# Compressor products with 128 moving columns, and the first block's projections from rows not yet normalised

## The reference, cut to what matters

```python
def first_block(x, norm1_g, w_in, ...):
    for i in range(DEPTH):                       # DEPTH = 2
        h = rmsnorm(x, norm1_g[i])
        mix = hybrid_mixer(h, w_in[i], cmp_pos[i], cmp_w1[i], cmp_w2[i], ...)
        x = x + mix @ w_out[i]
        h = rmsnorm(x, norm2_g[i])
        x = x + conv_glu_ffn(h, w_up[i], ...)
    return rmsnorm(x, final_g)
```

## Time and profile before

| | |
|---|---|
| median of 3 runs (lowest, highest) | 1905.39 us (1905.17 to 1916.05) |
| profiled execution, span from first to last instruction | 1924.8 us |
| time around that span | not shown; the profile has the span alone |
| mean granted PE clock in it | 0.986 |
| PE, PEld, DVE, ACT busy | 98%, 90%, 70%, 50% |
| records of all engines | 31636 |

### The profile page before, as it was taken

The page is one execution under the profiler, slowest core; times in us unless marked ns, Lnnn a source line. Parts: engine busy times, 40 slices in busy tenths (PEclk is TensorE's granted clock), DMA queues, the critical chain, the costliest instruction groups (busy, mean ns, idle before and its releaser), DMA issues.

```text
span 1924.8 us, 31636 instructions
## 1 busy us (share of the span) xinstructions
PE 1879.2 (98%) x12720; PEld 1726.5 (90%) x12720; DVE 1354.0 (70%) x2154; ACT 958.4 (50%) x1429; POOL 110.6 (6%) x112
## 2 busy tenths in 40 slices
PE   8999999999999999999999999999999999999998
PEld 6888999888899999999888989998999898989997
DVE  5566878745777787677877877777776777875445
ACT  5556444645654445434754454345343565454433
POOL 0000000000000000000001401100110001400100
PEclk9989999997999999999999999999999999999999
DMA  7215777541367777776431157875786442035552
GB/s 286 70 63 197 262 270 292 183 155 66 110 244 284 280 262 278 281 267 221 158 127 67 62 212 279 307 276 213 278 302 226 150 138 103 1 132 198 196 202 82
DMA packets 54510, 374.45 MB, mean 195 GB/s; under 512 B 6016, under 2 KB 6656, under 8 KB 12800
## 3 DMA queue, kind: packets, MB, share of 16 engines
q1 hardware_dynamic: 51808, 362.34, 51.3%
q0 software_dynamic: 2304, 9.93, 1.5%
q10 hardware_dynamic: 288, 0.65, 0.1%
HBM read 371.84 MB, written 1.05 MB: 194 GB/s over the span
## 4 chain that ended last, share of the span: by engine, by line
PE 87%; DVE 7%; ACT 4%; issue 1%; DMA 0%; SPq 0%; DVEq 0%; ACTq 0%
PE bank L707 14%; PE bank L709 14%; PE bank L708 14%; PE bank L870 6%; PE bank L871 6%; PE bank L872 6%; PE bank L783 3%; PE bank L784 3%; PE bank L785 3%; PE bank L1348 2%; DVE w_lo L1988 2%; PE bank L1358 1%; PE bank L1056 1%; PE bank L833 1%; PE bank L1025 1%
## 5 line engine op out<-in xcount | busy, mean ns | idle before, releaser
L1988 DVE TENSOR_TENSOR w_lo<-raw,w_hi 128x2048 fp32r<-128x2048 f32 (+4 forms) x279 | 607.8, 2182 | 76.4 <-ACT w_hi L1446 76.0
L707 PE MATMUL bank<-hT_hi,w_hi 128*128 128x256 f32 x2304 | 654.1, 284 | 2.0 <-DVE scratch L2747 2.0
L708 PE MATMUL bank<-hT_lo,w_hi 128*128 128x256 f32 x2304 | 651.8, 283 | 0.0
L709 PE MATMUL bank<-hT_hi,w_lo 128*128 128x256 f32 x2304 | 651.8, 283 | 0.0
L1446 ACT ACTIVATE w_hi<-raw 128x2048 fp32r<-128x2048 f32 (+4 forms) x268 | 502.1, 1875 | 147.5 <-PE bank L872 116.2
L707 PEld LDWEIGHTS bank<-hT_hi,w_hi 128*128 128x128 f32 x2304 | 440.1, 191 | 8.9 <-issue 6.5
L708 PEld LDWEIGHTS bank<-hT_lo,w_hi 128*128 128x128 f32 x2304 | 440.2, 191 | 2.8 <-issue 0.5
L709 PEld LDWEIGHTS bank<-hT_hi,w_lo 128*128 128x128 f32 x2304 | 440.2, 191 | 0.2
L870 PE MATMUL bank<-w_hi,hid_hi 128*128 128x512 f32 x528 | 206.7, 392 | 1.1 <-DVE hid_lo L2064 0.8
L871 PE MATMUL bank<-w_lo,hid_hi 128*128 128x512 f32 x528 | 206.2, 391 | 0.0
L872 PE MATMUL bank<-w_hi,hid_lo 128*128 128x512 f32 x528 | 205.4, 389 | 0.0
(11 more groups left out here) (410 smaller groups left out, 2451.2 us busy)
## 6 DMA issues: line engine op xcount, KB each, us to landing
raw<-in_wb SPq DMA_DIRECT2D x158, 1024.0 KB, 4.9
raw<-in_wa SPq DMA_DIRECT2D x94, 1024.0 KB, 4.9
scratch<-in_wm SPq DMA_DIRECT2D x72, 1024.0 KB, 7.0
raw<-in_wb SPq DMA_DIRECT2D x8, 940.0 KB, 4.7
raw<-in_wb SPq DMA_DIRECT2D x4, 936.0 KB, 4.7
lnw<-in_ln_g POOLq DMA_DIRECT2D x6, 512.0 KB, 5.0
lnw<-in_ln_b POOLq DMA_DIRECT2D x6, 512.0 KB, 6.1
scratch<-in_c SPq DMA_DIRECT2D x5, 512.0 KB, 3.7
```

The lines of the kernel that those rows point to most:

```text
L707: nc.tensor.matmul(out, ah, bh, start=(i == 0), stop=False)
L708: nc.tensor.matmul(out, ah, bl, start=False, stop=False)
L709: last = nc.tensor.matmul(out, al, bh, start=False, stop=(i == n - 1))
L1988: return nc.vector.tensor_tensor(w_lo[:, slot, cols], raw[:, raw_slot, cols], w_hi[:, slot, cols].bitcast(F32), ALU.subtract)
```

## The change

1. The compressor's first products take 128 moving columns in place of 30. The operand is a window of 128 columns of `rw`, which holds 32 x 30 columns side by side; the 30 that are wanted come first in it (for the last few products the window is clamped and the output shifted). The output window lies so that the wanted sums gather at columns 68 to 97 of the bank.
2. In the first block's input projection PE turns x and not `xn`; ACT's copies out of the banks multiply by the row factor. `rms_tile` of both row tiles moves on ACT from ahead of the first turned tiles to behind the splitting of both tiles for chunks 0 and 1, and so ahead of hi(2). DVE no longer writes `xn` there.
3. At the start of the program x is loaded by row tile, chunk 0 in two halves, and ACT and DVE split chunk 0 in four quarters; 18 idle transposes are dropped, 10 stay. The table of small parameters is loaded in three parts.
4. Between the layers, PE turns the first row tile two tiles of the sweep earlier, and the 8 idle transposes are dropped. The table load for the root at the end of layer 0 is dropped too.
5. The last chunk's copy out is two instructions of 256 columns and no longer one of 512. Some semaphores are merged.

```diff
@@ sync (SP): start of the program
-            sp.dma_start(x[:, :, :], t["x"].rearrange("o (t p) d -> p (o t) d", p=P)).then_inc(x_in, 16)
             sp.dma_start(cst[:, 0:P], t["const"][:, 0:P]).then_inc(x_in, 16)
+            sp.dma_start(x[:, 0, :], rows_of_x[:, 0, :]).then_inc(x_in, 16)
+            sp.dma_start(spa[:, 0:KT], t["sa"][0, :, 0:KT]).then_inc(small_in, 16)
+            sp.dma_start(raw[:, 0, 0:2 * HW], t["wa"][0, 0, :, 0:2 * HW]).then_inc(open_in, 16)
...
+                    if (l, n) == (0, 0):
+                        sp.dma_start(raw[:, 0, 2 * HW:CW], t["wa"][0, 0, :, 2 * HW:CW]).then_inc(raw_in[0], 16)
+                        sp.dma_start(x[:, 1, :], rows_of_x[:, 1, :]).then_inc(row_in, 16)
+                        continue
@@ tensor (PE): sweep, start of a layer, compressor
-                            if (i, half, f) == (1, 1, FT - 1) and turn_first is not None:
+                            if (i, half, f) == (1, 1, FT - 3) and turn_first is not None:
...
                 if l == 0:
-                    idle_turns(0, 18)
-                    pe.wait_ge(A["xn"], due(A, "xn", 1))
-                    turn_tile(A, xn, 0, 1)
+                    turn_tile(A, x, 0, 1)
+                    idle_turns(0, 10)
 
                 def turn_next():
-                    pe.wait_ge(A["xn"], due(A, "xn", 2 * TT + 2))
-                    turn_tile(A, xn, 0, 1)
+                    pe.wait_ge(A["x"], summed(l, 0, 1))
+                    turn_tile(A, x, 0, 1)
 
                 def turn_second():
-                    pe.wait_ge(A["xn"], due(A, "xn", TT))
-                    turn_tile(A, xn, 1, 1)
-
-                if l == 0:
-                    idle_turns(0, 10)
-                else:
-                    idle_turns(0, 8)
+                    if l == 0:
+                        pe.wait_ge(row_in, 16)
+                    else:
+                        pe.wait_ge(A["x"], summed(l - 1, 1, 1))
+                    turn_tile(A, x, 1, 1)
...
+                        elif l:
+                            pe.wait_ge(A["x"], summed(l - 1, 1, i))
...
-                        last = nc.tensor.matmul(G[0][:, 0:2 * NCMP], raw[:, n % RING, (first + jj) * P:(first + jj + 1) * P],
-                                                rw[:, j, :], start=(j == 0), stop=(j == CBLK - 1))
+                        at = min(j * 2 * NCMP, CBLK * 2 * NCMP - P)
+                        to = HID_AT - (j * 2 * NCMP - at)
+                        last = nc.tensor.matmul(G[0][:, to:to + P], raw[:, n % RING, (first + jj) * P:(first + jj + 1) * P],
+                                                lent[0][:, at:at + P], start=(j == 0), stop=(j == CBLK - 1), skip_group_check=True)
@@ scalar (ACT): start of a layer, copies out
                 if l == 0:
-                    hi_a(0)
-                    rms_tile(NEXT, 1, 3, lambda i, half: None)
                     act.wait_ge(small_in, 16)
-                    hi_tile(A, 0, 0, "g1", range(KH))
-                    hi_a(1)
-                    hi_tile(A, 0, 1, "g1", range(KH))
-                else:
-                    act.wait_ge(A["x"], summed(l - 1, 1, 0))
-                    square(NEXT, 1, 0)
-                    half_mean(NEXT, 1, 6 * l + 4)
-                    hi_tile(A, 0, 0, "g1", range(0, 2))
-                    act.wait_ge(A["x"], summed(l - 1, 1, 1))
-                    square(NEXT, 1, 1)
-                    root_mean(NEXT, 1, 6 * l + 6)
-                    hi_tile(A, 0, 0, "g1", range(2, KH))
-                    hi_a(1)
-                    hi_tile(A, 0, 1, "g1", range(KH))
+                    hi_tile(A, 0, 0, "g1", range(0, 2))
+                    hi_open(0)
+                    hi_open(1)
+                    hi_tile(A, 0, 0, "g1", range(2, KH))
+                    hi_open(2)
+                    hi_open(3)
+                else:
+                    hi_tile(A, 0, 0, "g1", range(KH))
+                hi_tile(A, 0, 1, "g1", range(KH))
+                hi_a(1)
                 for i in range(TT):
                     hi_tile(A, 0, i, "g1", range(KH, KT))
+                for i in range(TT):
+                    rms_tile(NEXT, i, 6 * l + 3 * i, lambda i, half: act.wait_ge(A["x"], summed(l - 1, i, half)) if l else None)
...
+                    act.wait_ge(A["rstd"], due(A, "rstd", i + 1))
+                    nc.scalar.activation(pj[:, i, WIN_A_AT[c]:WIN_A_AT[c] + WIN_A[c]], G[i][:, 0:WIN_A[c]], ACT.Copy,
+                                         scale=row_scale(i)).then_inc(A["pj"], 1)
...
-                load_table(ACT.Sqrt)
-                rms_tile(NEXT, 0, 6 * l + 6, lambda i, half: act.wait_ge(A["x"], summed(l, i, half)))
+                if l + 1 == DEPTH:
+                    load_table(ACT.Sqrt)
+                    rms_tile(NEXT, 0, 6 * l + 6, lambda i, half: act.wait_ge(A["x"], summed(l, i, half)))
@@ vector (DVE): start of a layer, end of layer 0
                 if l == 0:
-                    plain_row(0, 1, 1)
-                    lo_a(0)
-                    dve.wait_ge(small_in, 16)
                     lo_tile(A, 0, 0, "g1", range(0, 2))
-                    plain_row(1, 2, 2)
+                    lo_open(0)
+                    lo_open(1)
                     lo_tile(A, 0, 0, "g1", range(2, KH))
-                    lo_tile(A, 0, 1, "g1", range(KH))
-                    lo_a(1)
+                    lo_open(2)
+                    lo_open(3)
                 else:
+                    lo_tile(A, 0, 0, "g1", range(2, KH))
                     sums(l - 1, 1, 1)
...
+                lo_tile(A, 0, 1, "g1", range(KH))
+                lo_a(1)
                 for i in range(TT):
                     lo_tile(A, 0, i, "g1", range(KH, KT))
+                for i in range(TT):
+                    row_factor(i, TT * l + i + 1)
...
-                    plain_row(0, TT * l + TT + 1, 2 * TT * l + 2 * TT + 1)
+                    layer["first"] = l + 1
+                    lo_tile(A, 0, 0, "g1", range(0, 2))
```

More of the change, by code:

```diff
@@ L774, in token_chunk, with token_part @@
                 return last
-            def token_part(bank, i, slot, half, width, features=None, ks=range(KH)):
+            def token_part(bank, i, slot, half, width, features=None, ks=range(KH), weights=lambda k: None):
                 rows = slice(i * P, (i + 1) * P)
@@ L786, in token_part, with token_half @@
                 return last
-            def token_half(banks, slot, half, free, features=None, width=HW, between=lambda: None, amid=None):
+            def token_half(banks, slot, half, free, features=None, width=HW, between=lambda: None, amid=None, weights=lambda k: None):
                 for i in range(TT):
@@ L793, in token_half @@
                     if i == 0 and amid is not None:
-                        token_part(banks[i], i, slot, half, width, features, range(2))
+                        token_part(banks[i], i, slot, half, width, features, range(2), weights)
                         amid()
-                        last = token_part(banks[i], i, slot, half, width, features, range(2, KH))
+                        last = token_part(banks[i], i, slot, half, width, features, range(2, KH), weights)
                     else:
@@ L982, in _ @@
                 for c, width in enumerate(WIN_A[:2 * PAIRS_A]):
-                    pe.wait_ge(lo_done, split + (c + 1 + NEW))
+                    if (l, c) != (0, 0):
+                        pe.wait_ge(lo_done, split + (c + 1 + NEW))
                     def free(i, c=c):
@@ L987, in free @@
                             pe.wait_ge(A["pj"], due(A, "pj", c - 1 + i))
+                        elif l:
+                            pe.wait_ge(A["x"], summed(l - 1, 1, i))
                     token_half(G, c % RING, c % 2, free, (A, 0) if c < 2 else None, width, lambda c=c: between(c),
[L989 removed]
+                               None if c else turn_second, opening_weights if (l, c) == (0, 0) else lambda k: None)
                 c, width = 2 * PAIRS_A, LAST_A
@@ L1076, in compressed @@
                                                         start=True, stop=True)
-                        last.then_inc(A["cs"], 1)
+                        last.then_inc(A["by_pe"], 1)
                     if step == CPT_AT:
@@ L1091, in compressed @@
                                                     start=True, stop=True)
-                        last.then_inc(A["co"], 1)
+                        last.then_inc(A["by_pe"], 1)
                 pe.wait_ge(A["pj"], due(A, "pj", A_WIN))
@@ L1539, in ffn, with hi_open @@
                 post(FT - 1, 1, 1, FFN_N - 3, next_first)
-            rms_tile(NEXT, 0, 0, lambda i, half: None)
+            def hi_open(q):
+                cols = slice(q * HW, (q + 1) * HW)
+                act.wait_ge(open_in if q < 2 else raw_in[0], 16)
+                nc.scalar.activation(w_hi[:, 0, cols], raw[:, 0, cols], ACT.Copy).then_inc(open_hi if q < KH - 1 else hi_done, 1)
             for l in range(DEPTH):
@@ L1640, in _ @@
```

(23 more changed lines are left out.)

87 lines of the change are left out of this document (49 added, 38 removed).

## The result

| | before | after |
|---|---|---|
| median (lowest, highest), 20 runs each | 1905.24 us (1905.03, 1926.69) | 1915.99 us (1913.78, 1916.68) |
| profiled execution, span | 1924.8 us | 1913.1 us |
| mean granted PE clock in it | 0.986 | 0.995 |

The median rose by 10.75 us where 11.4 us less were forecast: direction and range are missed. Yet the two profiled spans differ by 1913.1 - 1924.8 = -11.7 us, the forecast sum to a tenth. Both are true, and the case is about why. The time around a span is 1914.93 - 1913.1 = 1.8 us, so the profiled execution of before took about 1926.6 us, 21.4 above the median.

What follows compares the result with a forecast made beforehand. PE was taken as the bound, with 48 us at half clock in two attention stretches. Terms -21.0 + 4.1 + 0.7 + 4.2 + 0.3 = -11.7 us on 1905.4 gave 1894 us; forecast's own range 1888 to 1901, eight-in-ten range 1885 to 1903.

Steps and rivals of the forecast that it cites:

- the base of the sum: Whole program: the summed -11.7 us, taken from the profiled execution, applied unscaled to the 1905.4 us median, giving 1894.
- first term: Compressor products in both layers' attention: 128 columns hold the clock at 1.00, saving 10.5 us a layer, 21.0 in all.
- rival (b): Attention steps 1 to 4: the width doesn't hold the clock, both stretches stay at half rate; +10.1 us, 1915.5; chance 0.1.
- Part 1: Compressor products widened to 128 columns: clock holds, 12.0 us a layer at most, 10.5 with DVE the later one.
- DVE list: DVE's work in attention steps 3 to 7: 3.44, 3.44, 2.0 and 3.2 us, turning 12 us saved into 10.5.
- Rival (a): Attention steps 5 to 7: PE pauses up to 1.9 us, clock falls all the same; 8 us dearer, 1902; chance 0.2.
- The load of the stationary operand: Compressor products: the load sets a record's time, 107 ns at full clock, 206 at half; the rule has 107 throughout.
- Part 2: Input projection: both roots hold ACT 4.9 us ahead of hi(2), delaying chunk 2 by 4.1 us in layer 1, 0.7 in layer 0.
- The clock behind the pauses: Chunk 2 in each layer: after a 5.5 us PE pause the clock falls, 2.1 us lost each, +4.2 us.
- Case (c): Pauses in front of chunk 2 don't cost the clock or are shorter; -17.6 us, 1888; chance 0.18.
- the rest: Last chunk's copy out in two instructions: +0.2 us a layer at most, 0.3 in all; semaphores, parameter table, earlier turn nothing.

Runs made afterwards that it cites:

- wide_only: The kernel before with the compressor's products at 128 columns in place of 30 and nothing else changed; 1905.17 us, ratio 0.999 to before.
- warm: The changed kernel with 46 idle transposes added in each pause ahead of chunk 2; 1910.43 us, ratio 1.0014 to before.
- narrow: The changed kernel with the compressor's products back at 30 columns; median 1920.67 us, six runs at 1914.4 to 1915.1 and six at 1926.2 to 1927.6.
- thin_twice: The kernel before with each of the compressor's products issued twice in succession at 30 columns; 1943.89 us, ratio 1.0197 to before.
- wide_twice: The kernel before with each of the compressor's products issued twice in succession at 128 columns; 1919.39 us, ratio 1.0067 to before.
- table_first: The changed kernel with the root's table loaded ahead of need in both layers, the roots left in place; 1912.21 us, ratio 1.0022 to before.

## Why the prediction was wrong

**The step that failed** is the base of the sum: "The saving is in waits and clock, not in proportion, so I apply it as it is: 1905.4 - 11.7 = 1894". The -21.0 us are taken from the two half-clock stretches of the profiled execution, and the median run of before has neither (wide_only: 0.0 us, and the 79 of 95 runs at 0.998). The prediction even wrote "That span is 19.4 us (1.0%) longer than the median of the runs; no run's profile tells why". The profile did: the prediction had priced each stretch at 10.5 us, two are 21.0, and the span was 19.4 above the median without the time around it. The three runs shown, two at 1905 and one at 1916.05, were one step of that size apart. The right sum had no first term: 1905.4 + 4.1 + 0.7 + 4.2 + 0.3 = 1914.7, with 1915.99 measured. Its own rival (b) comes to nearly the same (1915.5), but by luck: there the width failed to hold the clock, and it held.

**Part 1, mechanism and size: right where the stretches exist.** Logits of unit 0 to unit 7 take 107.15 - 88.56 = 18.6 us, and the same two stood 29.4 us apart in the trace of before (86.06 to 115.45): 10.8, where the prediction took 10.8 and booked 10.5. Here the forecast's DVE list is right to 0.1 us (11.95 us from unit 3 to unit 7, of 12.08). A record takes 111 to 115 ns from start to start, in place of the 110 expected. Rival (a) didn't come: PE's pause at unit 5's values is 1.28 us, not 1.9, and the clock stayed:

```profile
109.24 0.43 PE L1061 MATMUL bank<-scratch 128*128 128x64 f32 x2 [1.28 <-ACT scratch L1696]
```

**The load of the stationary operand** slows down with the clock. The 48 records of the slow stretch had 206 ns and have 111 to 115 now. The load's own records in before took 190 ns at the full clock and 333 in the slow stretch (shortest, middle and longest):

```profile
L1056 PEld LDWEIGHTS bank<-gateb,raw x128: 190/333/337, 87.1 to 461.9; 128*128 128x128 f32 x128
```

In the Trainium skill, the rule of "TensorE: Matmul & The Clock Gate", section "LDWEIGHTS" (columns over 1.2 GHz, with no word of the granted clock), would have left 4.8 us a layer out of this gain, an estimate. The 10.8 measured say that the row was the better guide.

**Part 2: right.** The roots take ACT 24.53 - 19.67 = 4.86 us (4.9). Chunk 2 of layer 0 comes at 28.94 against 28.22: +0.7, as forecast. By start times that vary with when the data land (28.94, 28.95 and 29.22 us in three traces with these roots) the tenth is luck. In layer 1, 379.27 - 372.33 = 6.9 us, of which layer 0 brings 0.7 + 1.9: +4.3 (4.1).

**The clock behind the pauses: right.** Two pauses of 5.4 us, 3.8 and 5.0 us at 0.50 behind them, 1.9 + 2.5 = 4.4 us (4.2). Case (c), in which they don't cost the clock or are shorter, is excluded by the windows of after, and warm shows that the pause is the cause. A slip without weight: the window at the end puts the fall 3.3 to 3.4 us behind PE's stop, not 3.6.

**Together** the terms measured in the traces are 0.7 + 1.9 + 4.3 + 2.5 = 9.4 us, and the spans of after and wide_only, which has all of before but the width, differ by 1913.1 - 1903.4 = 9.7. Since the 4.3 was itself taken as a remainder, the independent part of this agreement is what comes behind chunk 2 of layer 1: 2.8 us by the spans for the 2.5. The 0.3 left over equals what was booked for the rest, but no run separates that. The medians differ by 10.8, since the profiled run of after is 1.1 us below its median.

**What stays open:** why the same code keeps the clock in one run and loses it in another, and why the fall comes oftener with after's other parts (6 of 12 in narrow) than with before's (16 of 95). No run here tells it.

## What to carry to other kernels

Set the time of the profiled execution against the median of the runs before pricing anything in it: when they differ by about the price of a stretch that you mean to remove, and the runs stand in steps of that size, the median run may not have that stretch. A root or reduction that is moved behind a product isn't free because its result is needed late: here it stood in ACT's queue ahead of a split and a copy that PE was waiting for, and in the queue's gaps, with the table load and the first copy out moved too, next to nothing (1916.0 to 1901.1 us). In this kernel a pause of 4 to 5.5 us on PE cost twice, once as the pause and again by 2 us or so of half clock behind it.

## What the runs showed of the hardware that was not expected

- One program has three times, 10.8 us apart, by whether the clock falls in neither, one or both of two stretches of 24 us. By times and mean clocks it fell in 16 of 95 runs of before, in 6 of 12 of narrow and in all 4 of thin_twice; with 128 columns (wide_only, wide_twice, after and the six others built on it) in none of 102.
- The granted clock hides the slow start. Over before's first 18 transposes, 228 ns each, it reads 1.00; the 46 of warm take 113 ns each. PE's window of before (us, PE busy, clock, DMA share, GB/s), then warm:

```profile
6.00:10.00 4.00, 3.90 (x18) 1.00 1.03 422
```

```profile
24.34 5.18 PE L725 MATMUL bank<-cst 128*128 128x128 f32 x46
```

- ACT's first table load of the program started at 0.75 us in before, while the data were on their way. In after ACT first waits 6.29 us for the turned tile, and the load stands behind that wait; with the load back in front (table_first) chunk 1 started only 0.4 us earlier (17.42 for 17.83), not 1.28:

```profile
6.29 1.28 ACT L1505 ACT_TABLE_LOAD   x1 [6.29 <-PE bank L773]
```

- A copy out with a factor per row is dearer than one without: the two copies of pair (0,1) take 1.24 us in a row and took 1.07 before. The prediction put nothing for it.
